# The last part's first layer with 512 moving columns: both parts of x side by side for the 22 gate and up slabs

## Chip, cores, metric

One core of one Trainium2 chip (trn2). The metric is the device time of one execution in microseconds; the number compared is the median of several runs.

## What is computed

The program is a stack of transformer-like layers on 256 tokens of width 1024, all in float32: an attention layer with two mixers, an MLP, a dilated-attention layer, a second MLP, and then a second block of three branches, a merge and a gated feed-forward with a convolution over time. Only the feed-forward at the very end is touched here:

```python
h = rms_norm_2(x, ffn_norm_gain[l])
g = causal_dwconv(h @ w_ffn_gate[l], ffn_conv_w[l], ffn_conv_b[l])
x = x + (jax.nn.gelu(g) * (h @ w_ffn_up[l])) @ w_ffn_down[l]
return rms_norm_2(x, final_norm_gain)
```

`w_ffn_gate` and `w_ffn_up` are 1024 x 3072, `w_ffn_down` is 3072 x 1024, and the convolution has three taps.

## The kernel before

**Two parts for every operand.** A float32 product is made of products of a high and a low part: `whi` is the weight rounded to the matmul's own format, `wlo` the rest, and the same for x (`XHL` holds the high part in its columns 0 to 255 and the low part in 256 to 511, for each of 8 chunks of 128 rows). Three of the four products are made: high by high, low weight by high x, high weight by low x.

**Slabs.** All weights come in 192 slabs of 1 MB, each 128 x 2048 in SBUF. For slab n, SyncE loads `raw` (5 buffers); ScalarE (ACT) copies it to `whi` (3 buffers, line 1138, called `high`); then VectorE (DVE, line 1587) or, for the gate slabs, GpSimd (POOL, line 2316, four instructions of 512 columns) subtracts and writes `wlo` (5 buffers). `ahead(n)` in each engine's program does this for slab n + 2; `high(n + 2)` first waits until TensorE (PE) is through with slab n - 1, whose buffer it takes.

**The last part** has 12 pairs j = 0 to 11. Pair j has a gate slab, number FF + 2j, and an up slab, FF + 2j + 1; below they are counted 0 to 23 from FF, so that pair j has the slabs 2j and 2j + 1. After them come 12 slabs of `w_ffn_down`, the down slabs 0 to 11. `features` makes a slab's two halves m = 0, 1 (128 outputs each) in one bank of PSUM, each by 24 matmuls with 256 moving columns (line 538). After slabs 4, 8, 12 and 16 PE transposes a quarter of x for the end (`rows_in`, line 1105) and ACT copies it out (line 1542).

Each engine runs its instructions in the order in which the program is written. For pair j that order is:

- ACT: `high` for slab 2j + 2; `ffn_high(j - 1)`, the high part of the product z of the pair before (line 1530); `high` for slab 2j + 3; in four pairs the copy of `rows_in`; GELU of pair j (line 1545), which waits for DVE's convolution.
- DVE: z of pair j - 1 (line 2243, the GELU times the up slab straight from PSUM); the gate slab times the norm's factor out of PSUM (line 2223); three taps (lines 2229 and 2235, six instructions); `wlo` of slab 2j + 3; the low part of z, `HL` (line 2249).
- POOL: `wlo` of slab 2j + 2, as soon as its `whi` is there.

The two MLPs before this part already use another form, `beside`: a half m has its own bank, 8 matmuls take all 512 columns of `XHL` against `whi` (line 553), 8 take 256 columns against `wlo` (line 556); the two results lie in the bank's halves. ACT copies the second half to SBUF (`copies`, line 1197), DVE adds the first to it (`added`, line 1714).

Of the kernel before, what the change touches and what calls it, by code (L numbers as in the profile page):

```python
# [7 lines left out]
ALU = mybir.AluOpType  # L8
# [3 lines left out]
P = 128  # L12
S = 256
# [66 lines left out]
class Tally:  # L80
# [214 lines left out]
def build(nc, A, out):  # L295
    with ExitStack() as ctx:
# [214 lines left out]
        def w_ready(n, kc, c0, cols):  # L511
            hi, lo = whi_of(n), wlo_of(n)
            return [(hi[:, c, c0:c0 + cols], lo[:, c, c0:c0 + cols], ("whi", n), ("wlo", n)) for c in range(kc)]

        def tensor(pe):
# [3 lines left out]
            def bank(use):  # L519

                i = turn_no[0] % 8
                turn_no[0] += 1
                if used[i] is not None:
                    once.wait_ge(*at(("taken", *used[i])))
                used[i] = use
                bank_of[use] = i
                return ps[i]
# [11 lines left out]
                if event is not None:  # L539
                    m.then_inc(*tell(s_product, event))  # L540

            def beside(n, x, between=None):


                for m in range(2):
                    if m and between is not None:
                        between()
                    b = bank(("beside", n, m))
                    w = w_ready(n, 8, m * P, P)
                    for c in range(8):  # L550
                        for event in (w[c][2], x[c][2], x[c][3]):
                            once.wait_ge(*at(event))
                        pe.matmul(b[:, :], w[c][0], XHL[:, c, :], start=c == 0, stop=False)  # L553
                    for c in range(8):
                        once.wait_ge(*at(w[c][3]))
                        i = pe.matmul(b[:, 0:S], w[c][1], x[c][0], start=False, stop=c == 7)  # L556
                    i.then_inc(*tell(s_product, ("product", "beside", n, m)))
                released[n] = [("product", "beside", n, 1)]

            def features_low_last(n, x):  # L560
# [14 lines left out]
            def features(n, x, late=False, between=None):  # L575
                b = bank(("slab", n))
                for m in range(2):
                    if m and between is not None:
                        between()
                    product(b[:, m * S:m * S + S], w_ready(n, len(x), m * P, P), x, ("product", "slab", n) if m else None, late=late)  # L580
                released[n] = [("product", "slab", n)]
# [524 lines left out]
                m.then_inc(*tell(s_product, ("product", "rows", j)))  # L1106

            for n in range(FF + 2, FD):
                features(n, x)
                if n - FF in (4, 8, 12, 16):  # L1110
                    rows_in((n - FF - 4) // 4)

# [12 lines left out]
        def scalar(act):  # L1125
# [14 lines left out]
            def ahead(n):  # L1140
                for k in ahead_of(n):
                    high(k)
# [385 lines left out]
            def ffn_high(j):  # L1528
                once.wait_ge(*at(("ffn z", j)))
                act.activation(HH[:, 512 * j:512 * j + 512], TB[j % 2][:, :], ACT.Copy, scale=1.0).then_inc(*tell(s_xhi, ("hhi", 2, j)))  # L1530

            for j in range(12):
                ahead(FF + 2 * j)
                if j == 0:
                    root("n6", 0, cols=True)
                else:
                    ffn_high(j - 1)
                ahead(FF + 2 * j + 1)
                if j in (3, 5, 7, 9):
                    i = (j - 3) // 2  # L1540
                    b = take(("rows", i))
                    act.activation(XR[:, :, 256 * i:256 * i + 256], pair(b[:, :]), ACT.Copy, scale=1.0).then_inc(
                        *tell(s_act_out, ("taken", "rows", i)))
                once.wait_ge(*at(("ffn conv", j)))
                act.activation(TA[j % 2][:, :], TA[j % 2][:, :], ACT.Gelu_apprx_tanh).then_inc(*tell(s_act, ("ffn gelu", j)))
            ffn_high(11)

            def squared_rows(q, t):
# [30 lines left out]
        def vector(dve):  # L1579
# [639 lines left out]

            def ffn_conv(j):  # L2220
                y, s0 = pair(TA[j % 2][:, :]), pair(gv[j % 2])
                b = take(("slab", FF + 2 * j))
                dve.tensor_tensor(s0, pair(b[:, :]), twice(r6), ALU.mult).then_inc(*tell(s_dve_out, ("taken", "slab", FF + 2 * j)))
                once.wait_ge(*at(("taken", "slab", FF + 2 * j)))
                if j > 1:
                    once.wait_ge(*at(("ffn z", j - 2)))
                for m in range(2):
                    c = 2 * j + m
                    i = dve.tensor_scalar(y[:, m, :], s0[:, m, :], fcol("fcw", 48 + c), fcol("fcb", c), ALU.mult, ALU.add)
                i.then_inc(*tell(s_dve, ("ffn tap", j, 2)))  # L2230
                for k in (1, 0):
                    o = 2 - k
                    once.wait_ge(*at(("ffn tap", j, k + 1)))
                    for m in range(2):
                        i = dve.scalar_tensor_tensor(out=y[:, m, o:S], in0=s0[:, m, 0:S - o], scalar=fcol("fcw", 24 * k + 2 * j + m),
                                                     in1=y[:, m, o:S], op0=ALU.mult, op1=ALU.add)
                    i.then_inc(*tell(s_dve, ("ffn tap", j, k), *([("ffn conv", j)] if k == 0 else [])))

            def ffn_high(j):
                b = take(("slab", FF + 2 * j + 1), [("ffn gelu", j)])  # L2240
                if j > 1:
                    once.wait_ge(*at(("hlo", 2, j - 2)))
                dve.tensor_tensor(TB[j % 2][:, :], TA[j % 2][:, :], b[:, :], ALU.mult).then_inc(
                    *tell(s_dve_out, ("taken", "slab", FF + 2 * j + 1), ("ffn z", j)))

            def ffn_low(j):
                once.wait_ge(*at(("ffn z", j)))
# [297 lines left out]
```

## Time and profile before

| | us |
|---|---|
| median of 3 runs | 1227.53 (1226.71 to 1229.65) |
| the profiled execution, its own time | 1224.94 |
| its span | 1223.1 |
| PE busy | 1212.0 (99%) |
| DVE busy | 818.8 (67%) |
| ACT busy | 632.7 (52%) |
| POOL busy | 204.5 (17%) |
| chain that ended last | PE 90%, DVE 4%, ACT 2% |

The page sums each engine over the whole span. The chain is followed back from the last instruction to what released each step. The granted clock of TensorE in the profiled execution is 0.998 of full speed. Matmuls are pipelined and the busy times of neighbours overlap, so in a row of matmuls the time from one start to the next is what counts.

### The profile page before, as it was taken

How to read it: one execution, taken by the hardware profiler on the slowest of the kernel's cores; microseconds unless marked ns; L12 is line 12 of the kernel's file. 1: busy time of each engine (PE TensorE's matmuls, PEld its weight loads, DVE VectorE, ACT ScalarE, POOL GpSimd, SP SyncE). 2: the span in 40 equal slices, each digit the busy share in tenths (PEclk: the TensorE clock that was granted, in tenths of full speed). 3: DMA queues.
4: the chain of work that ended last, by engine and by line, in shares of the span. 5: the costliest groups of instructions: out<-in, count | busy, mean ns of one | idle time of the engine just before them, and what ended most of it. 6: DMA issues, size and time to landing. Idle time of an engine off the chain costs nothing.

```text
span 1223.1 us, 19863 instructions
## 1 busy us (share of the span) xinstructions
PE 1212.0 (99%) x8225; PEld 1093.4 (89%) x8225; DVE 818.8 (67%) x1127; ACT 632.7 (52%) x813; POOL 204.5 (17%) x160
## 2 busy tenths in 40 slices
PE   8999999999999999999999999999999999999998
PEld 8988898888899989999998888898878899999986
DVE  6878768754475665776879854587875577656643
ACT  5575465534455454445555543456576545444342
POOL 2600010000011201110310000010010795443100
PEclk9999999999999999999999999999999999999999
DMA  9723456565676555554355656555554555555551
GB/s 235 261 84 124 139 173 196 182 204 176 206 228 203 175 180 178 188 176 147 104 170 175 195 185 206 175 185 172 173 172 138 167 187 181 173 173 181 198 182 60
DMA packets 162074, 214.27 MB, mean 175 GB/s; under 512 B 5260, under 2 KB 117199, under 8 KB 161983
## 3 DMA queue, kind: packets, MB, share of 16 engines
q1 hardware_dynamic: 156574, 205.11, 52.0%
q10 hardware_dynamic: 5216, 7.42, 2.1%
q8 instruction: 65, 1.06, 0.4%
q0 software_dynamic: 192, 0.46, 0.1%
q14 instruction: 27, 0.21, 0.1%
HBM read 205.63 MB, written 1.05 MB: 169 GB/s over the span
## 4 chain that ended last, share of the span: by engine, by line
PE 90%; DVE 4%; ACT 2%; issue 2%; DMA 2%; SPq 0%; POOL 0%; ACTq 0%; DVEq 0%
PE ps L538 61%; PE ps L553 8%; PE ps L556 4%; PE ps L628 4%; PE ps L570 4%; PE ps L725 3%; PE ps L762 2%; PE ps L733 2%; DVE wlo L1587 1%; DMA raw<-in_ev_w_in_dram 1%; ACT whi L1138 1%; DVE XT L1728 0%; DMA TB<-TA 0%; DVE SN L1659 0%; PE ps L1014 0%
## 5 line engine op out<-in xcount | busy, mean ns | idle before, releaser
L1587 DVE TENSOR_TENSOR wlo<-raw,whi 128x2048 fp32r<-128x2048 f32 (+1 forms) x167 | 385.9, 2312 | 194.0 <-ACT whi L1138 193.7
L1138 ACT ACTIVATE whi<-raw 128x2048 fp32r<-128x2048 f32 x188 | 358.0, 1907 | 200.1 <-PE ps L538 179.3
L538 PE MATMUL ps<-XHL,whi 128*128 128x256 f32 x1552 | 280.6, 284 | 0.0
L538 PEld LDWEIGHTS ps<-XHL,whi 128*128 128x128 f32 x1552 | 240.6, 192 | 0.6 <-issue 0.4
L538 PE MATMUL ps<-XHL,wlo 128*128 128x256 f32 x776 | 212.8, 283 | 0.1
L538 PE MATMUL ps<-whi,HL 128*128 128x512 f32 (+1 forms) x416 | 148.7, 373 | 0.0
L538 PE MATMUL ps<-whi,HH 128*128 128x512 f32 x384 | 147.2, 390 | 0.0
L538 PEld LDWEIGHTS ps<-XHL,wlo 128*128 128x128 f32 x776 | 145.7, 192 | 0.4 <-DVE wlo L1587 0.3
L538 PE MATMUL ps<-whi,XHL 128*128 128x512 f32 (+1 forms) x576 | 145.3, 345 | 0.0
L538 PE MATMUL ps<-wlo,HH 128*128 128x512 f32 x368 | 143.2, 389 | 0.0
L2316 POOL TENSOR_TENSOR wlo<-raw,whi 128x512 fp32r<-128x512 f32 x88 | 115.3, 1343 | 142.9 <-ACT whi L1138 142.7
L553 PE MATMUL ps<-XHL,whi 128*128 128x512 f32 x448 | 112.4, 393 | 0.0
L538 PEld LDWEIGHTS ps<-whi,XHL 128*128 128x128 f32 x576 | 97.8, 190 | 12.3 <-issue 0.7
L538 PE MATMUL ps<-wlo,XHL 128*128 128x512 f32 (+1 forms) x288 | 96.4, 343 | 0.0
L2382 POOL TENSOR_TENSOR TB<-TB,BIG 128x512 f32<-128x512 f32 x24 | 34.7, 1447 | 361.6 <-DMA TB<-TA 361.6
L553 PEld LDWEIGHTS ps<-XHL,whi 128*128 128x128 f32 x448 | 80.6, 189 | 14.4
L1206 ACT ACTIVATE SN<-SN,stat 128x512 f32<-128x512 f32 (+2 forms) x64 | 38.2, 598 | 96.8 <-DVE stat L1659 94.3
L538 PEld LDWEIGHTS ps<-whi,HL 128*128 128x128 f32 x416 | 76.0, 188 | 13.6
L538 PEld LDWEIGHTS ps<-whi,HH 128*128 128x128 f32 x384 | 71.9, 188 | 14.6
L538 PEld LDWEIGHTS ps<-wlo,HH 128*128 128x128 f32 x368 | 69.1, 188 | 14.5
L556 PEld LDWEIGHTS ps<-XHL,wlo 128*128 128x128 f32 x448 | 61.0, 190 | 5.1 <-DVE wlo L1587 0.8
L556 PE MATMUL ps<-XHL,wlo 128*128 128x256 f32 x448 | 62.6, 282 | 0.3 <-DVE wlo L1587 0.3
(266 smaller groups left out, 1760.8 us busy)
## 6 DMA issues: line engine op xcount, KB each, us to landing
raw<-in_mlp_w_dram SPq DMA_DIRECT2D x64, 1024.0 KB, 5.2
raw<-in_od_w_in_dram SPq DMA_DIRECT2D x36, 1024.0 KB, 5.4
raw<-in_w_in_dram SPq DMA_DIRECT2D x24, 1024.0 KB, 5.1
raw<-in_w_ffn_gate_dram SPq DMA_DIRECT2D x12, 1024.0 KB, 5.2
raw<-in_w_ffn_up_dram SPq DMA_DIRECT2D x12, 1024.0 KB, 5.2
raw<-in_w_ffn_down_dram SPq DMA_DIRECT2D x12, 1024.0 KB, 5.1
TB<-TA ACTq DMA_DIRECT2D x96, 64.0 KB, 3.9
raw<-in_w_branch_dram SPq DMA_DIRECT2D x6, 1024.0 KB, 5.2
```

The source lines that it names most:

```text
L538: m = pe.matmul(to, l[c][a], r[c][b], start=first and k == 0, stop=last and k == 3 * n - 1)
L553: pe.matmul(b[:, :], w[c][0], XHL[:, c, :], start=c == 0, stop=False)
L556: i = pe.matmul(b[:, 0:S], w[c][1], x[c][0], start=False, stop=c == 7)
L570: i = pe.matmul(b[:, m * S:m * S + S], w[m][c][a], x[c][z], start=m == c == a == z == 0, stop=m == a == 1 and c == len(x) - 1)
L628: i = pe.matmul(b[n][:, m * S:m * S + S], h[a], x[c][z], start=m == c == a == z == 0, stop=m == 1 and c == 7 and z == 1)
L725: m = pe.matmul(banks[u][:, lo:hi], l, r, start=start, stop=stop)
L733: m = pe.transpose(b[:, to:to + P], SN[:, u % 3, of:of + P], ident[:, :])
L1138: act.activation(whi_of(n), raw_of(n), ACT.Copy, scale=1.0).then_inc(*tell(s_whi, ("whi", n)))
L1206: m = act.activation(SN[:, u % 3, lo:hi], src[:, lo:hi], ACT.Exp, bias=stat[:, u % 3, k:k + 1], scale=-1.0 if biased else 1.0, accum_out=s ...
L1587: dve.tensor_tensor(wlo_of(n), raw_of(n), f32(whi_of(n)), ALU.subtract).then_inc(*tell(s_wlo, ("wlo", n)))
L2316: m = pool.tensor_tensor(lo[:, v], r[:, v], f32(hi[:, v]), ALU.subtract)
L2382: pool.tensor_tensor(z, z, twice(RP[:, S:512]), ALU.mult).then_inc(*tell(s_pool, ("sine", k)))
```

## The change

The 22 slabs 2 to 23 of the last part go through `beside` in place of `features`. `beside` gets an argument `late`: for the gate slabs (whose low part POOL makes) both halves' high matmuls come ahead of both halves' low ones. ACT gets `copies` for both slabs of each pair: that of the up slab behind the next pair's first `high`, that of the gate slab behind the second, ahead of GELU. DVE's `added` writes the gate slab to SBUF, a second instruction multiplies it by the norm's factor there; the up slab is added into `TB`, and z is then made from two SBUF tensors. In pair 11 the `wlo` of down slab 1 moves ahead of the convolution.

```diff
-            def beside(n, x, between=None):
+            def beside(n, x, late=False):
...
+                high(0)
+                if not late:
+                    low(0)
+                high(1)
+                if late:
+                    low(0)
+                low(1)
                 released[n] = [("product", "beside", n, 1)]
...
             for n in range(FF + 2, FD):
-                features(n, x)
+                beside(n, x, late=pooled(n))
...
             for j in range(12):
                 ahead(FF + 2 * j)
+                if j > 1:
+                    copies(FF + 2 * j - 1, TB[(j - 1) % 2], *([("hlo", 2, j - 3)] if j > 2 else []))
...
+                if j:
+                    copies(FF + 2 * j, TA[j % 2], *([("ffn z", j - 2)] if j > 1 else []))
                 once.wait_ge(*at(("ffn conv", j)))
                 act.activation(TA[j % 2][:, :], TA[j % 2][:, :], ACT.Gelu_apprx_tanh).then_inc(*tell(s_act, ("ffn gelu", j)))
+            copies(FF + 23, TB[1], ("hlo", 2, 9))
             ffn_high(11)
...
+                if j:
+                    added(FF + 2 * j, gv[j % 2], TA[j % 2])
+                    dve.tensor_tensor(s0, s0, twice(r6), ALU.mult).then_inc(*tell(s_dve, ("ffn s", j)))
+                    once.wait_ge(*at(("ffn s", j)))
...
+                if j:
+                    added(FF + 2 * j + 1, TB[j % 2], TB[j % 2])
+                    once.wait_ge(*at(("ffn gelu", j)))
+                    dve.tensor_tensor(TB[j % 2][:, :], TA[j % 2][:, :], TB[j % 2][:, :], ALU.mult).then_inc(*tell(s_dve, ("ffn z", j)))
...
+                if j == 11:
+                    ahead(FF + 2 * j + 1)
                 ffn_conv(j)
-                ahead(FF + 2 * j + 1)
+                if j < 11:
+                    ahead(FF + 2 * j + 1)
```

How this moves instructions, on ACT in the middle of the last part. Before, from one GELU to the next (1138 is `high`, 1530 `ffn_high`, 1545 GELU):

```order
L1545 ACTIVATE TA<-TA 128x512
L1138 ACTIVATE whi<-raw 128x2048
L1530 ACTIVATE HH<-TB 128x512
L1138 ACTIVATE whi<-raw 128x2048
L1545 ACTIVATE TA<-TA 128x512
```

And in the changed kernel (1148 is `high`, 1207 `copies`, 1540 `ffn_high`, 1559 GELU):

```order
L1559 ACTIVATE TA<-TA 128x512
L1148 ACTIVATE whi<-raw 128x2048
L1207 ACTIVATE TB<-ps 128x256 x2
L1540 ACTIVATE HH<-TB 128x512
L1148 ACTIVATE whi<-raw 128x2048
L1207 ACTIVATE TA<-ps 128x256 x2
L1559 ACTIVATE TA<-TA 128x512
```

Two copies stand behind each of the two `high` instructions, and each has DVE's next step waiting for it.

On DVE in the same stretch, before (2223 reads the gate slab, 2229 and 2235 are the taps, 1587 `wlo`, 2249 `HL`, 2243 z):

```order
L2223 TENSOR_TENSOR SN<-ps,RS 128x512
L2229 TENSOR_SCALAR TA<-SN,FV 128x256 x2
L2235 SCALAR_TENSOR_TENSOR TA<-SN,FV,TA 128x255 x2
L2235 SCALAR_TENSOR_TENSOR TA<-SN,FV,TA 128x254 x2
L1587 TENSOR_TENSOR wlo<-raw,whi 128x2048
L2249 TENSOR_TENSOR HL<-TB,HH 128x512
L2243 TENSOR_TENSOR TB<-TA,ps 128x512
```

And changed (1729 is `added`, 2239 the factor, 2249 and 2255 the taps, 1602 `wlo`, 2272 `HL`, 2263 z):

```order
L1729 TENSOR_TENSOR SN<-ps,TA 128x256 x2
L2239 TENSOR_TENSOR SN<-SN,RS 128x512
L2249 TENSOR_SCALAR TA<-SN,FV 128x256 x2
L2255 SCALAR_TENSOR_TENSOR TA<-SN,FV,TA 128x255 x2
L2255 SCALAR_TENSOR_TENSOR TA<-SN,FV,TA 128x254 x2
L1602 TENSOR_TENSOR wlo<-raw,whi 128x2048
L2272 TENSOR_TENSOR HL<-TB,HH 128x512
L1729 TENSOR_TENSOR TB<-ps,TB 128x256 x2
L2263 TENSOR_TENSOR TB<-TA,TB 128x512
```

Four additions are new, and the factor and z now read SBUF alone.

On DVE at the end of the part, in the changed kernel, from the convolution of pair 10 (last row of the taps) to z of pair 11:

```order
L1602 TENSOR_TENSOR wlo<-raw,whi 128x2048
L2272 TENSOR_TENSOR HL<-TB,HH 128x512
L1602 TENSOR_TENSOR wlo<-raw,whi 128x2048
L1729 TENSOR_TENSOR TB<-ps,TB 128x256 x2
L2263 TENSOR_TENSOR TB<-TA,TB 128x512
L1602 TENSOR_TENSOR wlo<-raw,whi 128x2048
L1729 TENSOR_TENSOR SN<-ps,TA 128x256 x2
L2239 TENSOR_TENSOR SN<-SN,RS 128x512
L2249 TENSOR_SCALAR TA<-SN,FV 128x256 x2
L2255 SCALAR_TENSOR_TENSOR TA<-SN,FV,TA 128x255 x2
L2255 SCALAR_TENSOR_TENSOR TA<-SN,FV,TA 128x254 x2
L2272 TENSOR_TENSOR HL<-TB,HH 128x512
```

The third `wlo` (down slab 1) stood behind the taps before; it now stands ahead of the gate slab's addition.

## Rows read from the trace of the kernel before

**Rows 1.** Chain that ended last, last part: start us, us, what.

```profile
1020.54 20.26 PE ps L538 x168
1040.80 0.44 PE ps L1105 x4
1088.17 23.03 PE ps L538 x192
```

**Rows 2.** Timeline, PE in the first MLP: start, us, engine, line, what [idle before].

```profile
176.52 2.00 PE L553 MATMUL ps<-XHL,whi 128*128 128x512 f32 x8
178.36 1.12 PE L556 MATMUL ps<-XHL,wlo 128*128 128x256 f32 x8
179.31 2.00 PE L553 MATMUL ps<-XHL,whi 128*128 128x512 f32 x8
```

**Rows 3.** Timeline, ACT in the second MLP.

```profile
690.81 1.90 ACT L1138 ACTIVATE whi<-raw 128x2048 fp32r<-128x2048 f32 x1
692.62 0.36 ACT L1197 ACTIVATE TB<-ps 128x256 f32<-128x256 f32 x1
```

**Rows 4.** Timeline, DVE in the second MLP.

```profile
693.08 0.42 DVE L1714 TENSOR_TENSOR TA<-ps,TB 128x256 f32<-128x256 f32 x1
694.67 0.42 DVE L1714 TENSOR_TENSOR TA<-ps,TB 128x256 f32<-128x256 f32 x1 [1.17 <-ACT TB L1197]
695.13 0.69 DVE L1757 SCALAR_TENSOR_TENSOR TB<-TA 128x512 f32<-128x512 f32 x1
```

**Rows 5.** Timeline, DVE in the last part, pair 0.

```profile
1023.29 0.69 DVE L2223 TENSOR_TENSOR SN<-ps,RS 128x512 f32<-128x512 f32 x1
1024.02 0.74 DVE L2229 TENSOR_SCALAR TA<-SN,FV 128x256 f32<-128x256 f32 x2
1024.79 1.79 DVE L2235 SCALAR_TENSOR_TENSOR TA<-SN,FV,TA 128x255 f32<-128x255 f32 x4
1026.50 2.29 DVE L1587 TENSOR_TENSOR wlo<-raw,whi 128x2048 fp32r<-128x2048 f32 x1
1028.70 0.68 DVE L2243 TENSOR_TENSOR TB<-TA,ps 128x512 f32<-128x512 f32 x1
```

**Rows 6.** Timeline, ACT in the last part.

```profile
1026.62 0.63 ACT L1545 ACTIVATE TA<-TA 128x512 f32<-128x512 f32 x1 [2.05 <-DVE TA L2235]
1027.15 1.90 ACT L1138 ACTIVATE whi<-raw 128x2048 fp32r<-128x2048 f32 x1
1029.41 0.64 ACT L1530 ACTIVATE HH<-TB 128x512 fp32r<-128x512 f32 x1 [0.36 <-DVE TB L2243]
1029.95 1.90 ACT L1138 ACTIVATE whi<-raw 128x2048 fp32r<-128x2048 f32 x1
...
1076.25 1.92 ACT L1138 ACTIVATE whi<-raw 128x2048 fp32r<-128x2048 f32 x1 [3.33 <-PE ps L538]
1078.07 0.58 ACT L1542 ACTIVATE BIG<-ps 128x512 f32<-128x512 f32 x1
```

**Rows 7.** Timeline, POOL: the wlo of slab 4, one group of four instructions.

```profile
1029.20 5.34 POOL L2316 TENSOR_TENSOR wlo<-raw,whi 128x512 fp32r<-128x512 f32 x4 [6.64 <-ACT whi L1138]
```

**Rows 8.** Timeline, DVE ahead of the last part: one shape with POOL busy, then idle.

```profile
967.18 1.42 DVE L2156 TENSOR_TENSOR BIG<-BIG,TB 128x512 f32<-128x512 f32 x1
...
976.89 0.69 DVE L2156 TENSOR_TENSOR BIG<-BIG,TB 128x512 f32<-128x512 f32 x1
```

**Rows 9.** Timeline, POOL beside the first of these.

```profile
966.77 1.29 POOL L2316 TENSOR_TENSOR wlo<-raw,whi 128x512 fp32r<-128x512 f32 x1
```

**Rows 10.** The groups of instructions, last part: mean of that shape.

```profile
L2156 DVE TENSOR_TENSOR BIG<-BIG,TB 128x512 f32<-128x512 f32 x8 | 10.6, 1323 | 0.3
```

**Rows 11.** Timeline, ACT in the down slabs.

```profile
1157.45 1.92 ACT L1138 ACTIVATE whi<-raw 128x2048 fp32r<-128x2048 f32 x1 [2.06 <-PE ps L538]
1162.89 1.92 ACT L1138 ACTIVATE whi<-raw 128x2048 fp32r<-128x2048 f32 x1 [3.52 <-PE ps L538]
```

More of the change, by code:

```diff
@@ L540, in product, with high, low @@
                     m.then_inc(*tell(s_product, event))
-            def beside(n, x, between=None):
[L545 to L549, printed above, removed]
+            def beside(n, x, late=False):
+                b = {}
+                w = [w_ready(n, 8, m * P, P) for m in range(2)]
+                def high(m):
+                    b[m] = bank(("beside", n, m))
                     for c in range(8):
-                        for event in (w[c][2], x[c][2], x[c][3]):
+                        for event in (w[m][c][2], x[c][2], x[c][3]):
                             once.wait_ge(*at(event))
-                        pe.matmul(b[:, :], w[c][0], XHL[:, c, :], start=c == 0, stop=False)
+                        pe.matmul(b[m][:, :], w[m][c][0], XHL[:, c, :], start=c == 0, stop=False)
+                def low(m):
                     for c in range(8):
-                        once.wait_ge(*at(w[c][3]))
-                        i = pe.matmul(b[:, 0:S], w[c][1], x[c][0], start=False, stop=c == 7)
+                        once.wait_ge(*at(w[m][c][3]))
+                        i = pe.matmul(b[m][:, 0:S], w[m][c][1], x[c][0], start=False, stop=c == 7)
                     i.then_inc(*tell(s_product, ("product", "beside", n, m)))
+                high(0)
[5 more added lines that the diff above has]
+                low(1)
                 released[n] = [("product", "beside", n, 1)]
@@ L2221, in ffn_conv @@
                 y, s0 = pair(TA[j % 2][:, :]), pair(gv[j % 2])
-                b = take(("slab", FF + 2 * j))
-                dve.tensor_tensor(s0, pair(b[:, :]), twice(r6), ALU.mult).then_inc(*tell(s_dve_out, ("taken", "slab", FF + 2 * j)))
-                once.wait_ge(*at(("taken", "slab", FF + 2 * j)))
+                if j:
+                    added(FF + 2 * j, gv[j % 2], TA[j % 2])
+                    dve.tensor_tensor(s0, s0, twice(r6), ALU.mult).then_inc(*tell(s_dve, ("ffn s", j)))
+                    once.wait_ge(*at(("ffn s", j)))
+                else:
+                    b = take(("slab", FF))
+                    dve.tensor_tensor(s0, pair(b[:, :]), twice(r6), ALU.mult).then_inc(*tell(s_dve_out, ("taken", "slab", FF)))
+                    once.wait_ge(*at(("taken", "slab", FF)))
                 if j > 1:
@@ L2239, in ffn_high @@
             def ffn_high(j):
[L2240 to L2244, printed above, removed]
+                if j:
+                    added(FF + 2 * j + 1, TB[j % 2], TB[j % 2])
+                    once.wait_ge(*at(("ffn gelu", j)))
+                    dve.tensor_tensor(TB[j % 2][:, :], TA[j % 2][:, :], TB[j % 2][:, :], ALU.mult).then_inc(*tell(s_dve, ("ffn z", j)))
+                else:
+                    b = take(("slab", FF + 1), [("ffn gelu", 0)])
+                    dve.tensor_tensor(TB[0][:, :], TA[0][:, :], b[:, :], ALU.mult).then_inc(
+                        *tell(s_dve_out, ("taken", "slab", FF + 1), ("ffn z", 0)))
             def ffn_low(j):
```

## Prediction

> **What bounds the kernel now.** I read the chain of waits first. In the last part it holds nothing but TensorE: 192 matmuls (four slabs) take 23.03 us, and the transposes between 0.44 us [rows 1]. So PE is the bound, at 23.03 / 192 = 0.120 us a matmul, 48 x 0.120 = 5.76 us a slab. Only what makes PE faster, or makes it wait, counts. The timeline of an MLP, where `beside` already runs, shows its price: 8 wide matmuls take 178.36 - 176.52 = 1.84 us, 8 narrow ones 179.31 - 178.36 = 0.95 us [rows 2]. Then I read ACT, DVE and POOL in the timeline, to see when each slab's `whi` and `wlo` would be ready; starts are what counts there, since neighbours overlap.
>
> **PE alone.** A slab becomes 2 x (1.84 + 0.95) = 5.58 us in place of 5.76, a pair 11.17 in place of 11.52. For 22 slabs that is 22 x 0.175 = 3.85 us gained. The order of high and low halves in a gate slab changes no matmul's length.
>
> **ACT and DVE: a ring of waits.** Counted by engine nothing is full: ACT has some 6.3 us a pair, DVE 8.3 us, of 11.17. But the new order ties the two into one chain. From one GELU start to the next the changed kernel must do, in turn (starts to starts):
>
> - GELU 1027.15 - 1026.62 = 0.53, and `high` 1.81 behind it [rows 6, 3];
> - up slab's copies, additions, then z: first copy to first addition 0.46 to 0.49, the second addition some 0.35 behind (an estimate from 0.42 long instructions that overlap), the next instruction 695.13 - 694.67 = 0.46: together 1.30 [rows 3, 4];
> - z 0.69, to ACT 0.03: 0.71 [rows 5, 6]; `ffn_high` 0.54; `high` 1.81 again [rows 6, 3];
> - gate slab's copies and additions 1.30; factor 1024.02 - 1023.29 = 0.73; first tap 0.77; other taps to GELU 1026.62 - 1024.79 = 1.83 [rows 5, 6].
>
> The sum is 0.53 + 1.81 + 1.30 + 0.71 + 0.54 + 1.81 + 1.30 + 0.73 + 0.77 + 1.83 = 11.33 us, already over PE's 11.17. Before, GELU and z needed no copy and the first `high` was not in DVE's way, so the ring was not closed: DVE waited for PE in each pair.
>
> **What POOL adds.** `wlo` of the gate slab starts 1029.20 - 1027.15 = 2.05 us behind its `high` [rows 6, 7], that is 2.59 behind GELU, and lasts some 5 us. z stands at 0.53 + 1.81 + 1.30 = 3.64, inside. It used to read PSUM; now it reads two SBUF tensors, as line 2156 does ahead of the last part. That one takes 0.69 us with POOL idle and 1.42 beside it [rows 8], 1.32 as a mean [rows 10]. The single case shows how: POOL's instruction was over at 966.77 + 1.29 = 968.06 and DVE's at 968.60, 0.69 behind 967.91. So it waited until about 1.15 us after POOL's start, then ran at full speed, ahead of POOL's next one [rows 8, 9]. For z that gives 2.59 + 1.15 = 3.74, or some 0.1 later if `HL`, which runs at 2.1 to 2.8, holds POOL's first instruction up in its turn: 0.2 us of waiting. The Trainium skill (SBUF — State Buffer, "Who interferes with whom") says the same of the cause: a VectorE instruction with two SBUF inputs and a GpSimd one exclude each other for a whole instruction, and neither is merely slowed. The trace's single case agrees (1.42 = 0.73 waited + 0.69); a slowing by the mean, 1.32 for 0.69, would give the sum of the first rival below. POOL's last instruction ends about 8.2 behind GELU, just as the factor would start, so nothing more is added. I take a ring of **11.54 us**; the bounds are 11.33 (z never waits) and 11.33 + 0.68 = 12.01 (z takes double).
>
> **How the lag reaches PE.** Slab 2 starts on PE at 1020.54 + 24 x 0.12 = 1023.42 [rows 1]. GELU 1 follows from the rows too: `high` of slab 5 at 1029.95, copies at 1031.76, additions from 1032.25, factor ready to start at 1033.06; POOL's four instructions from 1029.20 [rows 6, 7] let it run at about 1034.1, so taps from 34.8 and GELU at 1037.4. `wlo` of slab 5 starts 0.12 ahead of it and is there 2.29 later, 1039.6. PE wants it at 1023.42 + 3 x 5.58 + 0.44 + 1.84 = 1042.4: 2.9 us of slack. Each pair then loses 11.54 - 11.17 = 0.37; up to pair 10 that is nine times, 3.3 us. ACT also has the four copies of `rows_in` inside the ring at 0.50 each (estimated from 0.58 less overlap), 2.0 us, where PE has three transposes more, 1.3 us. So 3.3 + 2.0 - 1.3 - 2.9 = **1.1 us** of waiting for `wlo` of up slabs, from about slab 19 on. `raw` loads are not late: they go on PE's own pace, as in the MLPs.
>
> **The end of the part.** Here is the larger term. Count from GELU 10. DVE: `wlo` of slab 23 at -0.12, `HL` 2.1, `wlo` of down slab 0 at 2.7 (each `wlo` holds DVE 2.20 [rows 5]), additions 4.9, z 5.7. ACT: `ffn_high` 6.4, `high` for down slab 1 at 6.95. DVE: its `wlo` at 9.0, which the change puts ahead of the convolution; additions 11.2, factor 12.0, taps 12.7 and 13.5. ACT: GELU 11 at 15.3, copies 15.8; DVE z 17.1; ACT `ffn_high` 17.85 and only then `high` of down slab 2 at 18.4: `whi` is there at 20.4, `wlo` at 22.7. PE: slab 23 gets its `wlo` at 2.2 and ends 0.95 + 1.84 + 0.95 later, at 5.9; two down slabs of 1162.89 - 1157.45 = 5.44 us [rows 11] bring it to 16.8. It waits 3.6 us for `whi`, then, having used it for two matmuls, 1.85 us for `wlo`: **5.45 us**. Behind that ACT and DVE are ahead again.
>
> **The sum.** -3.85 + 1.1 + 5.45 = +2.7 us. Against the profiled execution's own 1224.94 that is 1227.6; the median of the runs is 2.6 above that execution, so I forecast 1227.53 + 2.7 = **1230.2 us**. With the rest of the program unchanged, 0.3% is 3.7 us, about what a measurement of this kernel can tell from no change.
>
> **Rivals.**
>
> 1. *z takes double beside POOL.* For it: the mean of line 2156 [rows 10]. Against it: the single case [rows 8, 9]. The ring is 12.01, nine pairs lose 7.6, the waits become 5.4 and the sum -3.85 + 5.4 + 5.45 = +7.0: 1234.5 us. Should POOL win the next turn each time, z waits 1.24 more and the ring goes near 12.8: about +14, 1241.
> 2. *z never waits, or a link is shorter.* With 11.33 the nine pairs lose 1.4, 0.8 us of slack are left at slab 23 and the end costs 4.65: -3.85 + 4.65 = +0.8, 1228.3 us.
> 3. *Faster: PE stays the bound to the end.* Busy times speak for it (6.3 and 8.3 of 11.17 us), and the same `beside` runs without a wait in the MLPs. Its place is ACT's `high` of down slab 2: if that came by 14.7 behind GELU 10 in place of 18.4, no term but the first would be left, 1223.7 us. It decides at a ring under 11.17 and an end 5.5 us shorter. Against it stands the order itself: in the MLPs a pair has no GELU, no convolution and no POOL in the ring.
> 4. *The wide matmuls give nothing here*, since PE would stay at 5.76 us a slab: then the ring costs nothing on the way, slack is left at the end, and it comes out near +3, like the forecast. Rows 2 are against it.
>
> **Chances.** My own case, 1228.5 to 1232 (links uncertain by 0.1 us a pair, the end by 0.7): 0.52. Rival 1 with all above it: 0.25. Rival 2: 0.15. Rival 3: 0.05. Rival 4: 0.03. The range takes rival 2 with some room below and rival 1 with some above: **1226.5 to 1235.5 us**, leaving out the lost turn and rival 3. Faster by over 0.3% (under 1223.8): 0.05. Slower by over 0.3% (over 1231.2): rival 1 and nearly a quarter of my own case, 0.37. Within 0.3%: 0.58.
>
> **What the profile of the changed kernel would show.** PE at 11.17 us a pair with no gaps up to about slab 17, then gaps of some tenths ahead of the narrow matmuls of up slabs, released by DVE's `wlo`; GELU starts 11.5 us apart (12.0 where `rows_in` is copied); z at some 0.9 us; two gaps of 3.6 and 1.9 us at down slab 2, the first released by ACT. I am wrong in the ring if the GELUs stand 11.17 or over 11.8 apart without `rows_in`, in the end if no gap of over 2 us stands there, and in PE's price if a slab without waits is not 5.58.

## The result, and the profile after

In the comparison on one chip the changed kernel took 1228.86 us, median of 12 runs, the kernel before 1226.78 us (12 runs). One of the changed kernel's runs was disturbed (1985.81 us); the other eleven lie between 1226.83 and 1231.42 with a median of 1228.61, and only they count in the ratio. The ratio is 1.0026, with a 95% interval of 1.0014 to 1.0038. The changed kernel is a little slower, by 1.7 to 4.7 us; the middle of that interval is within 0.3% of no change, its upper end is not. The profiled execution took 1229.48 us (span 1227.7) against 1224.94.

Since single executions of one kernel differ by some us, I measured the part that the change touches in the traces: the **stretch**, from the start of the second half of slab 1 on PE to the start of the last matmul of the down slabs. It splits at the first matmul of down slab 0.

| kernel | up to down slab 0 | down slabs | stretch |
|---|---|---|---|
| before | 131.38 | 65.08 | 196.46 |
| changed | 127.87 | 72.20 | 200.07 |
| difference | -3.51 | +7.12 | +3.61 |

The stretch began 0.94 us later in the changed kernel's execution (1021.34 against 1020.40), in code that is the same; 0.94 + 3.61 = 4.55 is all of the 4.54 us between the two executions. In later runs the same point lay anywhere from 1018.1 to 1022.0, so 0.94 is scatter. (Some expectations below give the stretch as 196.3 and 199.9: they count from one matmul later.) Each stretch below comes from one profiled execution. Its first part repeats well: in the changed kernel and the five experiments that leave it alone it is 127.87 to 127.92.

The page of the changed kernel: busy times, then the chain that ended last.

```profile
PE 1212.1 (99%) x7873; PEld 1076.9 (88%) x7873; DVE 833.2 (68%) x1171; ACT 642.9 (52%) x857; POOL 208.7 (17%) x160
PE 78%; DVE 10%; ACT 5%; issue 3%; DMA 2%; SPq 0%; POOL 0%; ACTq 0%; DVEq 0%
```

PE is still busy for 99% of the span, but its part of the chain fell from 90% to 78%: the chain now runs through DVE and ACT from 1041.96 to 1165.78, over ten pairs. Where a busy share says "PE", the chain says "the ring", the loop of waits between ACT and DVE that the prediction added up.

Next the timeline of PE in up slab 21 (start, us, what), the counterpart of [rows 2].

```profile
1132.03 2.00 PE L553 MATMUL ps<-XHL,whi 128*128 128x512 f32 x8
1133.93 1.22 PE L558 MATMUL ps<-XHL,wlo 128*128 128x256 f32 x8
1134.99 2.00 PE L553 MATMUL ps<-XHL,whi 128*128 128x512 f32 x8
1136.83 1.12 PE L558 MATMUL ps<-XHL,wlo 128*128 128x256 f32 x8
```

The second half takes 1136.83 - 1134.99 = 1.84 and then 0.95 (the next slab starts at 1137.78), as in the MLP. The first takes 1134.99 - 1132.03 = 2.96 in place of 2.79: 0.17 us of waiting for `wlo`. In slab 23 it is 0.27. These two, 0.44 us, are all of the waiting on the way; -3.51 is -3.95 for PE alone and +0.44.

Now ACT for one turn of the ring, from one GELU to the next.

```profile
1108.37 0.63 ACT L1559 ACTIVATE TA<-TA 128x512 f32<-128x512 f32 x1 [3.94 <-DVE TA L2255]
1108.91 1.90 ACT L1148 ACTIVATE whi<-raw 128x2048 fp32r<-128x2048 f32 x1
1110.71 0.64 ACT L1207 ACTIVATE TB<-ps 128x256 f32<-128x256 f32 x2
1112.88 0.63 ACT L1540 ACTIVATE HH<-TB 128x512 fp32r<-128x512 f32 x1 [1.53 <-DVE TB L2263]
1113.41 1.90 ACT L1148 ACTIVATE whi<-raw 128x2048 fp32r<-128x2048 f32 x1
1115.22 0.63 ACT L1207 ACTIVATE TA<-ps 128x256 f32<-128x256 f32 x2
1119.79 0.63 ACT L1559 ACTIVATE TA<-TA 128x512 f32<-128x512 f32 x1 [3.94 <-DVE TA L2255]
```

DVE in the same turn:

```profile
1108.26 2.28 DVE L1602 TENSOR_TENSOR wlo<-raw,whi 128x2048 fp32r<-128x2048 f32 x1
1110.46 0.68 DVE L2272 TENSOR_TENSOR HL<-TB,HH 128x512 fp32r<-128x512 f32 x1
1111.18 0.76 DVE L1729 TENSOR_TENSOR TB<-ps,TB 128x256 f32<-128x256 f32 x2
1111.97 0.87 DVE L2263 TENSOR_TENSOR TB<-TA,TB 128x512 f32<-128x512 f32 x1
1115.68 0.75 DVE L1729 TENSOR_TENSOR SN<-ps,TA 128x256 f32<-128x256 f32 x2 [2.84 <-ACT TA L1207]
1116.47 0.69 DVE L2239 TENSOR_TENSOR SN<-SN,RS 128x512 f32<-128x512 f32 x1
1117.20 0.73 DVE L2249 TENSOR_SCALAR TA<-SN,FV 128x256 f32<-128x256 f32 x2
1117.96 1.79 DVE L2255 SCALAR_TENSOR_TENSOR TA<-SN,FV,TA 128x255 f32<-128x255 f32 x4
```

And POOL:

```profile
1110.95 5.56 POOL L2342 TENSOR_TENSOR wlo<-raw,whi 128x512 fp32r<-128x512 f32 x4 [6.36 <-ACT whi L1148]
```

Neither engine waits for PE anywhere in the turn; each waits only for the other. From GELU to GELU it is 11.42 us: 0.54 + 1.80 + 1.26 (copies and additions) + 0.91 (z, to `ffn_high`) + 0.53 + 1.81 + 1.25 + 0.73 + 0.76 + 1.83. With the copy of `rows_in` it is 11.91. z takes 0.87 and not 0.69: less 0.69 its end is at 1112.15, 1.20 behind POOL's start, the same phase as the 1.15 worked out from [rows 8, 9].

One link of the ring has two ways that are almost equally long. The up slab's additions at 1111.18 come 0.47 behind the first copy, but DVE itself is busy with `wlo` and `HL` from 1108.26 to 1111.14, and could have started them only about 0.1 us sooner (in a later kernel the additions start 0.60 behind `HL`, which gives 1111.06). The profile's chain goes this second way, by DVE's `wlo` and `HL`. So taking GELU and the first `high` out of the ring would bring only 0.1 us.

The end of the part, on PE:

```profile
1159.89 0.39 PE L538 MATMUL ps<-wlo,HH 128*128 128x512 f32 x1
1163.47 0.77 PE L538 MATMUL ps<-whi,HH 128*128 128x512 f32 x1 [3.20 <-ACT whi L1148]
1164.04 0.63 PE L538 MATMUL ps<-whi,HL 128*128 128x512 f32 x1
1165.78 0.79 PE L538 MATMUL ps<-wlo,HH 128*128 128x512 f32 x1 [1.11 <-DVE wlo L1602]
1166.37 0.63 PE L538 MATMUL ps<-whi,HH 128*128 128x512 f32 x1
1166.80 0.63 PE L538 MATMUL ps<-whi,HL 128*128 128x512 f32 x1
```

A matmul here follows the one before it after 0.227 us. So down slab 2 was due at 1160.12 and began 3.35 us late, for want of `whi`; its first `wlo` matmul came another 1.85 us late. Then comes something that I had not forecast: the matmuls stand 0.43 us apart in place of 0.227. The windows say why (length, busy times of PE, PEld, DVE, ACT, POOL, granted clock, DMA share, GB/s):

```profile
1160.00:1164.00 4.00, 0.80 (x3) 0.50 (x2) 2.09 (x4) 3.10 (x3) 0.00 (x0) 0.85 0.61 201
1164.00:1168.00 4.00, 2.89 (x7) 1.82 (x6) 4.00 (x3) 2.93 (x2) 0.00 (x0) 0.50 0.17 65
```

Behind the gap the granted clock is 0.50 of full speed, 1.2 GHz: by the clock's own records it fell at 1162.76, still within the first gap, stayed there for 6.8 us, and was back at 1.00 at 1169.59. The other executions show it too: over the whole span the mean clock is 0.996 or 0.997 in all eleven undisturbed ones of the changed kernel. Of the 7.12 us that the down slabs cost, 3.35 + 1.85 = 5.20 are the two waits and 1.92 the slow clock.

### The profile page after: what moved, and what is told of

It reads as the page before. It is cut to its first block, busy times and chain, and to the rows that moved or that the text cites. A ratio compares the mean times of both kernels' runs of the same rounds, so it can differ in the third digit from the quotient of the medians.

```text
span 1227.7 us, 19290 instructions
## 1 busy us (share of the span) xinstructions
PE 1212.1 (99%) x7873; PEld 1076.9 (88%) x7873; DVE 833.2 (68%) x1171; ACT 642.9 (52%) x857; POOL 208.7 (17%) x160
## 3 DMA queue, kind: packets, MB, share of 16 engines
q10 hardware_dynamic: 5216, 7.42, 2.1%
## 4 chain that ended last, share of the span: by engine, by line
PE 78%; DVE 10%; ACT 5%; issue 3%; DMA 2%; SPq 0%; POOL 0%; ACTq 0%; DVEq 0%
PE ps L538 49%; PE ps L553 9%; PE ps L558 5%; PE ps L638 4%; ACT whi L1148 3%; DVE wlo L1602 3%; PE ps L735 3%; PE ps L772 2%; PE ps L743 2%; PE ps L580 2%; DVE TA L2255 1%; DMA raw<-in_ev_w_in_dram 1%; DMA TB<-TA 1%; DVE TB L2263 1%; DVE TA L2249 1%
## 5 line engine op out<-in xcount | busy, mean ns | idle before, releaser
L553 PE MATMUL ps<-XHL,whi 128*128 128x512 f32 x800 | 198.8, 393 | 0.0
L553 PEld LDWEIGHTS ps<-XHL,whi 128*128 128x128 f32 x800 | 144.5, 189 | 26.4
L538 PE MATMUL ps<-XHL,whi 128*128 128x256 f32 x848 | 152.9, 285 | 0.0
L2342 POOL TENSOR_TENSOR wlo<-raw,whi 128x512 fp32r<-128x512 f32 x88 | 119.4, 1388 | 142.1 <-ACT whi L1148 141.8
L538 PEld LDWEIGHTS ps<-XHL,whi 128*128 128x128 f32 x848 | 130.5, 191 | 0.6 <-issue 0.4
L558 PEld LDWEIGHTS ps<-XHL,wlo 128*128 128x128 f32 x800 | 107.4, 190 | 8.3 <-DVE wlo L1602 1.5
L538 PE MATMUL ps<-XHL,wlo 128*128 128x256 f32 x424 | 113.2, 283 | 0.1
L558 PE MATMUL ps<-XHL,wlo 128*128 128x256 f32 x800 | 110.1, 283 | 0.3 <-DVE wlo L1602 0.3
L538 PEld LDWEIGHTS ps<-XHL,wlo 128*128 128x128 f32 x424 | 78.2, 192 | 0.3 <-DVE wlo L1602 0.3
```

The costliest lines, as they stand in the source:

```text
L538: m = pe.matmul(to, l[c][a], r[c][b], start=first and k == 0, stop=last and k == 3 * n - 1)
L553: pe.matmul(b[m][:, :], w[m][c][0], XHL[:, c, :], start=c == 0, stop=False)
L558: i = pe.matmul(b[m][:, 0:S], w[m][c][1], x[c][0], start=False, stop=c == 7)
L2342: m = pool.tensor_tensor(lo[:, v], r[:, v], f32(hi[:, v]), ALU.subtract)
```

## The experiments

**Theory A**, as the trace left it: (1) the ring of ACT and DVE, 11.42 us, is slower than PE's 11.17 and makes the waits of the last up slabs; (2) at the end, `whi` of down slab 2 waits on ACT behind GELU 11 and the z of pair 11, and the order of the instructions there makes both waits; (3) the slow clock follows from the gap. **Rivals**: the ends of the engines are late for another reason, so that the waits move on when they are taken away; ACT and DVE wait for PE and not PE for them; the slow clock comes by itself in this place. None of the kernels leaves out part of the computation.

### Both orders at the end put right

ACT makes the `whi` of down slabs 2 and 3 ahead of GELU 11, DVE their `wlo` ahead of and behind the convolution of pair 11.

```diff
@@ ACT, ahead of GELU j
+                if j == 11:
+                    ahead(FD)
+                    ahead(FD + 1)
@@ ACT and DVE, behind the last pair
-            for k in range(6):
+            for k in range(2, 6):
@@ DVE, pair j
                 if j == 11:
                     ahead(FF + 2 * j + 1)
+                    ahead(FD)
                 ffn_conv(j)
-                if j < 11:
+                if j == 11:
+                    ahead(FD + 1)
+                else:
                     ahead(FF + 2 * j + 1)
```

> The changed kernel with the high and low parts of down slabs 2 and 3 made ahead of GELU 11 and of the last z, nothing else. Theory A (the change gains 3.9 us on PE, loses about 0.4 to waits in the ring, and at the end loses 5.2 us of waiting at down slab 2 plus 1.9 us because PE then runs at the granted clock 0.5 for some us): both gaps at down slab 2 and the slow stretch go, from the second half of slab 1 to the last matmul it takes 196.3 - 3.5 = 192.8 us in place of 199.9 (before: 196.3), the granted clock stays 1.00 up to the last matmul, and the time is some 7 us under the change and 3.5 under before. Rival B (the end is late anyway, since the last z now comes later still): a gap of several us appears at down slab 3, 4 or 5 in its place, and the stretch stays near 199 us.

Measured: 1220.79 us, ratio 0.9966 (0.9955 to 0.9978). The stretch is 192.98, 7.09 shorter than the changed kernel's, with the down slabs at 65.08 exactly as before. The clock stayed at 1.00. ACT at the end:

```profile
1150.99 1.92 ACT L1148 ACTIVATE whi<-raw 128x2048 fp32r<-128x2048 f32 x1
1153.47 1.92 ACT L1148 ACTIVATE whi<-raw 128x2048 fp32r<-128x2048 f32 x1 [0.55 <-PE ps L538]
1159.33 0.63 ACT L1562 ACTIVATE TA<-TA 128x512 f32<-128x512 f32 x1 [3.94 <-DVE TA L2258]
```

The two `high` instructions lie in time in which ACT had nothing to do. GELU 11 comes 17.6 us behind GELU 10 (15.25 in the changed kernel), and nobody waits for it: z of pair 11 is first used by down slab 5, which starts 27 us behind down slab 0. So the order makes both waits, and this version is faster than both kernels. Whether ACT's order alone does it is the next question.

### Only ACT's order put right

As above on ACT, DVE's order left as in the changed kernel.

```diff
@@ ACT, ahead of GELU j
+                if j == 11:
+                    ahead(FD)
+                    ahead(FD + 1)
@@ ACT, behind the last pair
-            for k in range(6):
+            for k in range(2, 6):
```

> The changed kernel with only ACT's order changed at the end: the high parts of down slabs 2 and 3 ahead of GELU 11; DVE's order is left. Theory A (both waits come from one order on two engines; whi alone is half of it): no wait for whi; DVE makes the wlo of down slab 2 only behind HL, done some 4.4 us after PE wants it (from the changed kernel's trace: HL 1161.63, wlo 1162.25 to 1164.5 against 1160.5), so one wait of about 4.0 us for wlo in place of 3.4 + 1.9, and the slow clock behind it: stretch 200.07 - 1.2 = 198.8 us. Rival B (ACT's late high part was the whole cause, DVE only followed it): both waits gone, 193 to 194.5 us. Rival C (the two high parts ahead of GELU delay it so that nothing is gained): 200 or more.

Measured: 1226.34 us, ratio 1.0009 (0.9997 to 1.002); stretch 198.75, against 198.8 expected. PE and, in the second fence, DVE:

```profile
1160.98 0.39 PE L538 MATMUL ps<-whi,HL 128*128 128x512 f32 x1
1165.24 0.50 PE L538 MATMUL ps<-wlo,HH 128*128 128x512 f32 x1 [3.87 <-DVE wlo L1605]
```

```profile
1162.30 0.69 DVE L2275 TENSOR_TENSOR HL<-TB,HH 128x512 fp32r<-128x512 f32 x1 [0.77 <-ACT HH L1540]
1162.91 6.68 DVE L1605 TENSOR_TENSOR wlo<-raw,whi 128x2048 fp32r<-128x2048 f32 x3
```

`whi` is in time, and the wait moves to `wlo`: 4.03 us in one piece (due 1161.21), and 5.77 - 4.03 = 1.74 us of slow clock behind it. In this kernel the `wlo` stands behind `HL`, and `HL` behind `ffn_high`. So the second engine's order was a cause of its own, hidden behind the first: part (2) holds for the two orders together, not for ACT's alone.

### The moved low part back behind the convolution

```diff
-                if j == 11:
-                    ahead(FF + 2 * j + 1)
                 ffn_conv(j)
-                if j < 11:
-                    ahead(FF + 2 * j + 1)
+                ahead(FF + 2 * j + 1)
```

> The changed kernel with one part undone: the low part of down slab 1 stands behind the convolution of pair 11 again. Theory A (the end is one chain, and VectorE is two or three us late whichever comes first): PE waits 3.5 to 4 us for that low part at down slab 1 and then some 1.5 us more at down slab 2, where the changed kernel waits 3.4 and 1.9 at down slab 2; the stretch takes 199 to 200.5 us, as in the change. Rival B (moving it ahead is what makes the end late, as it holds the convolution up by two us): the stretch is 2 us shorter, 198.

Measured: 1226.7 us, ratio 1.0017 (1.0007 to 1.0028); stretch 198.16, 1.91 shorter than the changed kernel's. That is the number of rival B, but not its reason. PE now waits one slab earlier, at down slab 1, once:

```profile
1153.62 0.39 PE L538 MATMUL ps<-whi,HL 128*128 128x512 f32 x1
1157.39 0.79 PE L538 MATMUL ps<-wlo,HH 128*128 128x512 f32 x1 [3.39 <-DVE wlo L1602]
```

That is 3.54 us of waiting, and the slow matmuls behind it take 5.17 - 3.54 = 1.63 us longer. GELU 11 does come earlier (13.31 behind GELU 10, not 15.25), but DVE then makes the `wlo` of down slab 1 ahead of z, and for down slab 2 almost nothing is gained (ACT, then DVE):

```profile
1159.90 1.90 ACT L1148 ACTIVATE whi<-raw 128x2048 fp32r<-128x2048 f32 x1
```

```profile
1161.90 2.29 DVE L1602 TENSOR_TENSOR wlo<-raw,whi 128x2048 fp32r<-128x2048 f32 x1 [1.11 <-ACT whi L1148]
```

This `wlo` ends at 1164.19, 22.33 behind GELU 10; in the changed kernel it is 22.59. PE uses it at 1164.44, 5.16 late, against 5.20 in the changed kernel. So the end is one chain in both, as Theory A says, and the 1.9 us between them are the slow clock: here it falls into time in which PE would have had to wait for down slab 2 in any case, in the changed kernel it comes behind the last wait and is added to it.

### The ring made longer

The first experiment's kernel, with one more DVE instruction of 0.7 us between factor and taps, which leaves the numbers as they are.

```diff
+                    dve.tensor_tensor(s0, s0, s0, ALU.max).then_inc(*tell(s_dve, ("ffn s again", j)))
+                    once.wait_ge(*at(("ffn s again", j)))
```

> As e1, with one more VectorE instruction of 0.7 us in pairs 1 to 11 between the factor and the taps (the maximum of the slab with itself, which changes no number). VectorE has some 2.8 us free in a pair. Theory A (ring): GELU starts stand 11.42 + 0.73 = 12.15 us apart, once the slack of 3 us is gone PE runs at the ring's pace, and the stretch takes 192.8 + 7 = 199 to 201 us. Rival B (what counts is how busy an engine is): the free time takes it, and the stretch stays at 192.8 to 193.5 us.

Measured: 1227.48 us, ratio 1.0022 (1.0013 to 1.0031); stretch 200.40. That is 7.42 us more than without it, on average 0.67 for each of 11 pairs, nearly the whole instruction, though DVE is busy for only 68% of the changed kernel's span. Waits of PE (engine, line and releaser: us, times, longest), then the GELUs:

```profile
PE ps L558 <- DVE wlo L1605: 5.7, 7, 1.2
```

```profile
1111.48 0.63 ACT L1562 ACTIVATE TA<-TA 128x512 f32<-128x512 f32 x1 [4.67 <-DVE TA L2260]
1123.64 0.64 ACT L1562 ACTIVATE TA<-TA 128x512 f32<-128x512 f32 x1 [4.67 <-DVE TA L2260]
```

The GELUs stand 12.16 us apart in place of 11.42, and PE waits from about 1076 on. (The view counts only the time in which nothing runs; from start to start these seven matmuls come 0.9 to 1.4 us late, and the one behind each another 0.1.) Part (1) holds; by busy time the instruction would have been free.

### The ring made shorter, or so I thought

The copies go ahead of the `high` in each pair, in the first experiment's kernel.

```diff
             for j in range(12):
-                ahead(FF + 2 * j)
                 if j > 1:
                     copies(FF + 2 * j - 1, TB[(j - 1) % 2], *([("hlo", 2, j - 3)] if j > 2 else []))
+                ahead(FF + 2 * j)
...
+                if j:
+                    copies(FF + 2 * j, TA[j % 2], *([("ffn z", j - 2)] if j > 1 else []))
                 ahead(FF + 2 * j + 1)
...
-                if j:
-                    copies(FF + 2 * j, TA[j % 2], *([("ffn z", j - 2)] if j > 1 else []))
```

> As e1, and in each pair ACT makes its two copies ahead of the high part, not behind it. Theory A (two high instructions of 1.81 us stand in the ring of waits, which at 11.4 us is longer than PE's 11.17): without them in front of the copies the ring is shorter than PE, GELU starts stand 11.17 us apart (11.6 with a transpose), the additions wait for PE and not for ACT, no narrow matmul of an up slab waits, and the stretch takes 192.4 us, 0.4 under e1. Rival B (high parts must come first, or PE waits for its weights): whi comes later by the two copies, gaps stand ahead of the wide matmuls, and the stretch is longer than e1's by one us or more.

Measured: 1220.6 us, ratio 0.9963 (0.995 to 0.9975); stretch 192.51, no waits left. That is 0.47 less than the first experiment, the size of the waits. But the ring did **not** get shorter: the GELUs stand 11.41 apart in every pair. DVE and POOL in one pair:

```profile
1080.99 2.28 DVE L1605 TENSOR_TENSOR wlo<-raw,whi 128x2048 fp32r<-128x2048 f32 x1
1083.19 0.68 DVE L2275 TENSOR_TENSOR HL<-TB,HH 128x512 fp32r<-128x512 f32 x1
1083.79 0.75 DVE L1732 TENSOR_TENSOR TB<-ps,TB 128x256 f32<-128x256 f32 x2
1084.57 1.48 DVE L2266 TENSOR_TENSOR TB<-TA,TB 128x512 f32<-128x512 f32 x1
1087.09 0.76 DVE L1732 TENSOR_TENSOR SN<-ps,TA 128x256 f32<-128x256 f32 x2 [1.04 <-ACT TA L1207]
1087.88 1.13 DVE L2242 TENSOR_TENSOR SN<-SN,RS 128x512 f32<-128x512 f32 x1
1089.04 1.59 DVE L2252 TENSOR_SCALAR TA<-SN,FV 128x256 f32<-128x256 f32 x2
```

```profile
1084.22 5.93 POOL L2348 TENSOR_TENSOR wlo<-raw,whi 128x512 fp32r<-128x512 f32 x4 [5.46 <-ACT whi L1148]
```

z, the factor and the first taps now fall into POOL's `wlo` and take 1.48, 1.13 and 1.59 us in place of 0.69, 0.69 and 0.73: 2.1 us a pair of waiting for POOL, where the first order had 0.2, at z. The 1.9 us more eat up the second `high`, 1.81, which did leave the ring. The first `high` brings only 0.1: the up slab's additions come 1083.79 - 1081.10 = 2.69 us behind GELU, held by DVE's own `wlo` and `HL`, in place of 1111.18 - 1108.37 = 2.81. That both orders come out at 11.4 is chance. z less 0.69 began at 1085.36, 1.14 behind POOL's start, the phase of [rows 8, 9] once more. What did go is the copy of `rows_in`: it no longer lengthens its pair, 4 x 0.5 us, and that took away the waits.

### Copies first, the end unchanged

The same edit, in the changed kernel.

```diff
-                ahead(FF + 2 * j)
                 if j > 1:
                     copies(FF + 2 * j - 1, TB[(j - 1) % 2], *([("hlo", 2, j - 3)] if j > 2 else []))
+                ahead(FF + 2 * j)
...
```

> The changed kernel with its copies ahead of the high parts in each pair, and the end as in the change. From e2 both theories know that the ring is 11.41 us with the copies first as well, since z, the factor and the first tap then collide with POOL. Theory A (the two orders differ by 0.5 us on the way, the end is the same chain): no wait at up slabs, at down slab 2 gaps of some 3.5 and 1.9 us and the slow clock behind them, stretch 199.6 us. Rival B (without high parts in front of the copies the end's chain is shorter by a high part or more): the gaps shrink to 2 us or less and with them the slow clock, stretch 196 us or less.

Measured: 1226.1 us, ratio 1.001 (1.0 to 1.0021); stretch 196.51, of which the down slabs 69.08.

```profile
1158.49 0.47 PE L538 MATMUL ps<-whi,HH 128*128 128x512 f32 x1 [1.87 <-ACT whi L1148]
1160.80 0.50 PE L538 MATMUL ps<-wlo,HH 128*128 128x512 f32 x1 [1.60 <-DVE wlo L1602]
```

The ring hands on 2 us less of lag, the last pair is 0.95 longer (GELU 11 is 16.2 behind GELU 10), so both waits together are 4.0 us, all of 69.08 - 65.08: in this execution the clock stayed at 1.00. That is nearer to rival B (196 or less) than to Theory A (199.6). But this execution was the fastest of the ten, 1222.71 us, and it is not typical: its mean clock is 1.000, in the other nine it is 0.996 or 0.997, as in the changed kernel. Those nine have no trace, so where their clock fell and how long their gaps were isn't shown. Only for this one execution is it known that two gaps of 2.0 us left the clock alone.

### The order of high and low halves

With `late=False` for every slab, in the changed kernel:

```diff
-                beside(n, x, late=pooled(n))
+                beside(n, x, late=False)
```

> The changed kernel with one part undone: in the gate slabs too each half's low matmuls stand behind its own high ones. Theory A (the ring of ACT and VectorE sets when low parts come; the gate slab's comes from POOL 8 us behind its GELU and PE wants it only 11 us later): PE waits a little for POOL's low part late in the part, in all no more than 0.5 us more than the change waits there, and as the ring sets the end the stretch stays within 0.3 us of 200.1. Rival B (low last is what lets POOL keep up): waits of about 1 us at each of the last gate slabs, stretch over 202 us.

One execution: 1226.8 us, stretch 200.04. PE's weight loads wait 0.5 us for POOL's `wlo` once, and that is taken back at the end. And with `late=True` for every slab, in the first experiment's kernel:

```diff
-                beside(n, x, late=pooled(n))
+                beside(n, x, late=True)
```

> As e1 (the end's high and low parts ahead), and the up slabs too have their low matmuls last. Theory A: the low part of an up slab is wanted 1.84 us later, so the 0.45 us of waits at slabs 21 and 23 go, and the stretch takes 192.5 us, 0.45 under e1, as with the copies first. Rival B: as the ring runs at 11.42 us whatever PE does, the wait only moves to the low part of down slab 1, and the stretch stays at 193.0.

Measured: 1219.72 us, ratio 0.9961 (0.9946 to 0.9976); stretch 192.39, with 0.2 us of waiting left. The up slabs are the ones whose low part comes last in the ring; there the late order takes away the 0.44 us of waits. It also makes a slab itself a little shorter, 5.57 us in place of 5.59, which is another 0.2 us for the 11 up slabs. This is the shortest of all by its stretch, though the three kernels between 1219.7 and 1220.8 us can't be told apart by their times.

### The gap filled on PE

To see whether the slow clock follows from the gap, PE gets products of ones ahead of down slab 2, into a bank that nothing reads: first 28, then 14, in the changed kernel.

```diff
                 for k in range(6):
+                    if q == 0 and k == 2:
+                        i = turn_no[0] % 8
+                        once.wait_ge(*at(("taken", *used[i])))
+                        for _ in range(28):
+                            pe.matmul(ps[i][:, 0:P], ones[:, :], ones[:, :], start=True, stop=True)
```

> The changed kernel with 28 small matmuls of ones by ones (128 columns, some 0.11 us each, result unused) ahead of down slab 2 on PE, in the time in which PE waits there for the high part (3.4 us). Nothing is made earlier. Theory A (the wait itself costs 5.2 us, and 1.9 us more come from PE running at the granted clock 0.5 behind the gap): the gap is filled, the granted clock stays 1.00, the wait of 1.9 us for the low part stays, and the stretch from the second half of slab 1 to the last matmul takes 200.1 - 1.9 = 198.2 us. Rival B (the slow matmuls behind the gap come from the late low part or from DMA or VectorE load, not from the gap): they stay at 0.43 us a matmul, and the stretch at 200 us or more.

> The changed kernel with 14 small matmuls of ones ahead of down slab 2 on PE, into a bank that nothing reads (each ran as two of 0.11 us in the run with 28), so some 3.1 us of filler, which ends a few tenths ahead of whi. The waits for whi and wlo (3.4 and 1.9 us) stay as they are, but PE no longer stands still in the first. Theory A (the slow clock follows a gap of over 3 us on PE and adds 1.9 us): granted clock 1.00 all through, stretch from slab 1's second half to the last matmul 200.07 - 1.88 = 198.2 us, the second gap of 1.1 to 1.9 us left open. Rival B (the clock falls from something else in this place, or from the second gap too): slow matmuls and 200.0 us again.

Measured with 28: 1226.62 us, ratio 1.0019 (1.001 to 1.0029); stretch 199.29. With 14: 1227.43 us, ratio 1.0013 (0.9999 to 1.0026); stretch 198.35. PE, with 28:

```profile
1157.87 6.41 PE L1131 MATMUL ps<-ones 128*128 128x128 f32 x56
1164.04 0.48 PE L538 MATMUL ps<-whi,HH 128*128 128x512 f32 x1
```

and with 14:

```profile
1157.95 3.29 PE L1131 MATMUL ps<-ones 128*128 128x128 f32 x28
1161.30 0.47 PE L538 MATMUL ps<-whi,HH 128*128 128x512 f32 x1
1163.61 0.50 PE L538 MATMUL ps<-wlo,HH 128*128 128x512 f32 x1 [1.60 <-DVE wlo L1607]
```

Window behind them, with 14:

```profile
1164.00:1170.00 6.00, 6.00 (x28) 4.97 (x27) 3.96 (x2) 1.84 (x2) 0.00 (x0) 1.00 0.05 2
```

The 28 were a filler of my own mis-sizing: each ran as two instructions, 6.17 us in all, which outlasted both waits and held PE up by about another 1 us. Still the stretch is shorter than the changed kernel's. The 14 end just as `whi` is there (ACT starts it at 1159.27), the wait for `wlo` is left open, the clock stays at 1.00, and the stretch is 198.35 where 200.07 - 1.92 = 198.15 was to be had. So work that computes nothing makes this stretch 1.7 us shorter, by the clock alone. The times of the runs are too coarse to show it: both ratios overlap the changed kernel's.

The clocks of the other executions say how far this goes. With 28, which leave no gap, all ten have a mean of 0.998 to 1.000, against 0.996 or 0.997 in the changed kernel. With 14, which leave the second gap of 1.9 us open, six of ten have 0.999 or 1.000 and four have 0.997 or 0.998 (so have 4 of the 19 executions of the kernel before in that comparison). Part (3) holds: in the same place, with `whi` and `wlo` as late as before, there is no slow clock when PE doesn't stand still. Whether the second gap alone can bring it in some executions is open.

## Why the prediction was right, and where its terms were off

The forecast was 1230.2 us, +2.7 over before; the runs say 1228.86, +2.1 by the medians, +3.2 by the ratio, +3.61 by the stretches. It lies within my own case and on its side. Of the 1.3 us between 1230.2 and 1228.86, 0.75 come from the base: I started from a median of 3 runs, 1227.53, and 12 give 1226.78.

- **PE alone, -3.85.** Right: -3.95. A slab without waits takes 5.57 us with the low matmuls last and 5.59 by halves; the order, which I put at nothing, is worth 0.02 us a slab.
- **The ring, 11.54.** Right in kind, as the chain shows and the longer ring confirms; 11.42 in size. I took GELU, `high` and copy as the only way to the up slab's additions; DVE's own `wlo` and `HL` are as long to 0.1 us, and I had not counted them. The failing links are the two of copies and additions, 1.26 and 1.25 in place of 1.30 each (a pair of additions and the next instruction overlap more than my estimate of 0.35 + 0.46), and `high`, 1.80, and the first tap, 0.76. z cost what the exclusion gave, 0.91 against 0.71 + 0.2.
- **The waits of up slabs, 1.1.** 0.44. Nine pairs by 0.12 us make 1.1 us less lag, which by my own sum leaves 0.04. That 0.44 are there has a likely cause, which no run tests alone: a weight load starts ahead of its matmul, 0.22 us where nothing waits (1142.54 and 1142.77 in the kernel with the copies first), so `wlo` is wanted that much sooner than I put it. In slab 23 the load started at 1145.35, 0.05 behind the end of its `wlo` and 0.39 late. Place (slabs 21 and 23) and releaser were right.
- **The end, 3.6 + 1.85 = 5.45.** 3.35 + 1.85 = 5.20, with the engines and the order as forecast.
- **What was left out: 1.92 us.** I added the waits up and took every matmul behind them at full speed. The slow clock behind the gap is a term of its own, a third of the waits again. About half of it, 1.0, was made up by the two terms that I had too large (0.66 + 0.25) and by PE's 0.1; the other 0.9 is the difference between +2.7 and the +3.61 of the stretches. The right total is partly luck in that.
- **Rival 1** (z double) would have shown a ring of 12.0; in the changed kernel it is 11.42. What it would have cost is seen in the kernel with a ring of 12.16: 7.4 us more on PE. **Rival 2** (z never waits, or a link is shorter): its first half is refuted by z's 0.87, its second half is true by 0.12 us a turn, and its 1228.3 is nearer to the measured 1228.86 than my 1230.2. Its end of 4.65 is not what was measured (5.20), and it too leaves out the slow clock. **Rival 3** needed a ring under 11.17 and an end 5.5 us shorter. The first experiment built the second of these alone, with the ring still at 11.42, and it gave what the rival said: 1220.79 against 1224.79 for the kernel before on the same chip, -4.0, and -3.48 by the stretch. **Rival 4** is refuted by PE's slabs.
- I priced the end as one sum and never asked what the moved `wlo` alone does to it. In waits it brings next to nothing (5.20 us late with it, 5.16 without), and it puts the slow clock behind the last wait: 1.9 us lost.

## What to carry to other kernels

Count the ring of waits between two engines, link by link and start to start, not their busy time: here two engines at 52% and 68% set the pace, and 0.7 us more in the ring cost 7.4. At each step look for the second way to it: an instruction that leaves the ring brings only what the next longest way allows. Where one stage hands over to the next, look at what stands ahead of the next stage's operands in every engine's order; it took a few lines on ACT and on DVE, and ACT's alone brought 1.3 us of the 7.1. And behind the waits of 3.4 to 4.0 us on PE the clock was lower for some us, which cost extra unless PE would have had to wait in that time anyway. A profile is one execution: compare its clock with those of the others before reading a rule from it.

## What the runs showed of the hardware that I had not expected

- Behind a gap on PE of 3.35, 3.54 and 4.03 us the matmuls that followed were slower for a while, 0.43 us apart in place of 0.227, and granted 0.50 for 6.8, 3.4 and 3.4 us. The matmuls took 1.92, 1.63 and 1.74 us longer by it. In the first of these a second gap followed. The clock fell 0.7 and 0.3 us before PE went on in the first two, and 1.3 us after it in the third. In one profile two gaps of 2.0 us had no slow clock, but the nine other executions of that kernel have a mean clock of 0.996 or 0.997, so no bound can be read from these runs.
- A DVE instruction on two SBUF tensors that meets POOL's `wlo` starts about 1.15 to 1.20 us behind POOL's start and then runs at full speed, in the kernel before, the changed one and the one with the copies first. POOL pays too: its four instructions take 5.56 us with z's wait of 0.2 and 5.93 with the longer ones. Instructions with a scalar operand are held up as well: 1.59 against 0.73 us for the two of line 2252. Moving them into POOL's time can eat all that was gained by moving them earlier.
- A matmul of 128 columns of float32 ones shows as two instructions of 0.11 us each.
